# Second output projection: the order in which weight slabs are split and the residual is worked on

## What is computed

```python
merged = jax.nn.sigmoid(ga) * (ya @ w_branch_a[l]) + jax.nn.sigmoid(gb) * (yb @ w_branch_b[l])
h = h + merged @ w_out[l]                                     # the second output projection
h = h + 0.5 * swiglu(rms_norm(h, ffn2_norm[l]), ffn2_w_gate[l], ffn2_w_up[l], ffn2_w_down[l])
```

## Time and profile before

| | us |
|---|---|
| median of 3 runs | 1691.95 |
| lowest, highest | 1689.49, 1692.52 |
| the profiled execution, whole | 1687.92 |
| its span (first to last instruction) | 1686.0 |
| PE busy in the span | 1656.9 |
| DVE busy | 1038.9 |
| ACT busy | 738.2 |
| POOL busy | 177.9 |

### The profile page before, as it was taken

The page is one execution under the profiler, slowest core; times in us unless marked ns, Lnnn a source line. Parts: engine busy times, 40 slices in busy tenths (PEclk is TensorE's granted clock), DMA queues, the critical chain, the costliest instruction groups (busy, mean ns, idle before and its releaser), DMA issues.

```text
span 1686.0 us, 24849 instructions
## 1 busy us (share of the span) xinstructions
PE 1656.9 (98%) x9737; PEld 1415.5 (84%) x9737; DVE 1038.9 (62%) x1594; ACT 738.2 (44%) x1246; POOL 177.9 (11%) x185
## 2 busy tenths in 40 slices
PE   7999999999999998999999999999999999999998
PEld 5777687888888888989999887777888899998997
DVE  4888856443343376866767635666455687586773
ACT  3565644222222274524445422555444554253553
POOL 0120210020000012010000231002001200101102
PEclk9999999999999999999999999999999999999999
DMA  9733136373243378484565146112336975537721
GB/s 335 242 128 120 44 116 212 105 195 98 68 134 100 109 175 183 106 203 123 156 159 153 49 131 121 52 57 67 88 94 167 225 174 137 147 83 199 176 88 51
DMA packets 291463, 226.27 MB, mean 134 GB/s; under 512 B 16251, under 2 KB 275767, under 8 KB 291335
## 3 DMA queue, kind: packets, MB, share of 16 engines
q1 hardware_dynamic: 261056, 181.43, 34.6%
q0 software_dynamic: 29936, 43.18, 14.3%
q10 hardware_dynamic: 360, 0.13, 0.0%
HBM read 215.27 MB, written 6.36 MB: 131 GB/s over the span
## 4 chain that ended last, share of the span: by engine, by line
PE 56%; DVE 2%; ACT 1%; DMA 1%; issue 1%; POOL 0%; DVEq 0%; ACTq 0%; POOLq 0%
PE psum L698 10%; PE psum L700 10%; PE psum L699 10%; PE psum L1044 8%; PE psum L1047 8%; PE psum L1046 8%; PE psum L1192 1%; PE psum L1157 1%; DMA acc<-sq 1%; PE psum L1212 1%; DVE ring_lo L2211 0%; DVE w_lo L1971 0%; ACT ring_hi L1645 0%; DVE part_raw L2219 0%; PE psum L1130 0%
## 5 line engine op out<-in xcount | busy, mean ns | idle before, releaser
L2211 DVE TENSOR_TENSOR ring_lo<-part_raw,ring_hi 128x1024 fp32r<-128x1024 f32 (+1 forms) x270 | 323.4, 1199 | 200.6 <-ACT ring_hi L1645 199.7
L1645 ACT ACTIVATE ring_hi<-part_raw 128x1024 fp32r<-128x1024 f32 (+1 forms) x270 | 278.6, 1036 | 362.0 <-PE psum L700 286.3
L1044 PE MATMUL psum<-hq_hi,ring_hi 128*128 128x256 f32 x1232 | 350.3, 284 | 1.7 <-ACT t_gate L1736 1.2
L1046 PE MATMUL psum<-hq_lo,ring_hi 128*128 128x256 f32 x1232 | 349.1, 283 | 0.0
L1047 PE MATMUL psum<-hq_hi,ring_lo 128*128 128x256 f32 x1232 | 349.1, 283 | 0.0
L1044 PEld LDWEIGHTS psum<-hq_hi,ring_hi 128*128 128x128 f32 x1232 | 237.1, 192 | 3.0 <-issue 1.8
L1046 PEld LDWEIGHTS psum<-hq_lo,ring_hi 128*128 128x128 f32 x1232 | 237.1, 192 | 0.2
L1047 PEld LDWEIGHTS psum<-hq_hi,ring_lo 128*128 128x128 f32 x1232 | 237.0, 192 | 0.0
L698 PE MATMUL psum<-hid_hi,ring_hi 128*128 128x512 f32 (+1 forms) x536 | 207.2, 386 | 0.0
L699 PE MATMUL psum<-hid_lo,ring_hi 128*128 128x512 f32 (+1 forms) x536 | 206.9, 386 | 0.0
L700 PE MATMUL psum<-hid_hi,ring_lo 128*128 128x512 f32 (+1 forms) x536 | 206.8, 386 | 0.0
(11 more groups left out here) (305 smaller groups left out, 2418.7 us busy)
## 6 DMA issues: line engine op xcount, KB each, us to landing
part_raw<-in_ffn_w_up SPq DMA_DIRECT2D x66, 512.0 KB, 5.6
w_raw<-in_w_in SPq DMA_DIRECT2D x50, 512.0 KB, 3.7
part_raw<-in_w_gate_up SPq DMA_DIRECT2D x44, 512.0 KB, 4.9
part_raw<-in_ffn_w_gate SPq DMA_DIRECT2D x44, 512.0 KB, 6.9
part_raw<-in_ffn_w_down SPq DMA_DIRECT2D x32, 512.0 KB, 5.1
part_raw<-in_ffn_w_gate POOLq DMA_DIRECT2D x22, 512.0 KB, 7.0
part_raw<-in_ffn_w_up POOLq DMA_DIRECT2D x22, 512.0 KB, 9.9
sq<-in_w_ada SPq DMA_DIRECT2D x20, 512.0 KB, 4.6
```

Of the source, the lines that this page charges most:

```text
L1044: pe.matmul(o, a_hi, b_hi, start=fresh, stop=False, skip_group_check=True)
L1046: pe.matmul(o, a_hi, b_lo, start=False, stop=False, skip_group_check=True)
L1645: act.activation(ring_hi[slot][:, 0:n], pool_raw[s_][b][:, 0:n], ACT.Identity).then_inc(f_high, 1)
L2211: dve.tensor_tensor(ring_lo[slot][:, 0:n], raw_[:, 0:n], ring_hi[slot][:, 0:n].bitcast(F32), ALU.subtract).then_inc(f_ready, 1)
```

## The change

In the loop over tiles of out2, the split of a slab moves one tile forward. Before, iteration i began with the split of slab i+1 on ACT and on DVE. Now iteration 0 still splits slab 1, and then each iteration i up to 5 splits slab i+2. On ACT this stands at the head of iteration i, ahead of the split for the FFN, of the wait for x and of the work on h; it waits until PE has left slab i, which is when tile i is complete. On DVE it stands right behind the addition to x of tile i, ahead of `combos`. Iterations 6 and 7 split no slab.

```diff
@@ ScalarE @@
             for i, n in enumerate(PAIRED):
-                if i < KD - 1:
-                    split_high(S_OUT2 + i + 1)
+                if i == 0:
+                    split_high(S_OUT2 + 1)
+                if i < KD - 2:
+                    split_high(S_OUT2 + i + 2)
                 if i in AHEAD:
                     high(FIRST_ITEM[2] + AHEAD.index(i))
                 wait_new("out2", i, None, 1)
@@ VectorE @@
             for i, n in enumerate(PAIRED):
-                if i < KD - 1:
-                    split_low(S_OUT2 + i + 1)
+                if i == 0:
+                    split_low(S_OUT2 + 1)
                 b = wait_filled(dve, ("out2", i))
                 dve.tensor_tensor(x[:, n, :], psum[:, b, :], x[:, n, :], ALU.add).then_inc(x_new, 1)
+                if i < KD - 2:
+                    split_low(S_OUT2 + i + 2)
                 combos(n, "ffn2", NEW_X["out2"] + i + 1, col_of("ffn2_norm_2", n, None, 1),
                        lambda: lower(FIRST_ITEM[2] + AHEAD.index(i)) if i in AHEAD else None)
             lower(FIRST_ITEM[2] + 3)
```

## The result

| | before | changed |
|---|---|---|
| median | 1690.96 us (5 runs) | 1699.59 us (5 runs) |
| lowest to highest | 1689.49 to 1692.52 | 1697.87 to 1700.2 |
| profiled execution, span | 1686.0 | 1696.3 |
| PE busy | 1656.9 | 1661.3 |
| mean granted clock of PE | 0.997 | 0.992 |

The ratio on record is 1.0038, with a 95% interval of 1.0021 to 1.0055: slower, where the forecast was no change, and outside the range of 1688.0 to 1695.6. The medians differ by 8.6 us; their quotient is 1.0051, inside the interval but not the recorded ratio.

What follows compares the result with a forecast made beforehand. PE was taken to bound the kernel, with POOL's path nearly as long: -4.15 (stalls) + 1.05 (slab 7) + 3.0 (gather wait) + 0.9 (clock) = +0.8 us, so 1692.8 against the median 1691.95; range 1688.0 to 1695.6.

Steps and rivals of the forecast that it cites:

- the two paths: Up to 1345.09 us, PE's own path and one from the squares through POOL's queue were claimed nearly equal in length.
- The stalls of 4.15 us: PE's waits for late slabs in the out2 stage, claimed to cost 4.15 us and to go with the change.
- The split on PE's path: In out2, a split would end 2.5 us after its tile, against 5.44 for the next tile: no stall if slabs landed.
- slab 3: Its load would land only at 1295.1, holding ACT and DVE in its split; gather 1 moves from 1296.75 to 1300.75.
- the lag: Lateness of ACT, DVE and POOL after slab 3's split; DVE's falls over later tiles, tile 6 added at about 1323.3.
- The stall ahead of slab 7: Square of tile 4 waits for gather 2, delaying slab 7's split: PE stalls 0.9 us, plus 0.15 in slow matmuls.
- "POOL's order stays, and I take the durations of its DMAs unchanged.": POOL's gathers and adds keep order and durations; its path stays equal within 0.1 us, PE's gather wait grows to 3.6.
- slab 6 and POOL's adds: Slab 6, now issued at 1302.5 ahead of the adds at 1305.0, was taken to load in under 8 us, not 10.6.
- The bounds: Slab 6 at 10.6 us delays the last gather 1.4; slab 3 later adds 0.5; faster POOL gains 1.2; clock 0 or 1.1.
- rival (b), slower by late slabs: Slab 6 or 7 still moving blocks ACT in out2: +3.0 to +4.6 us, about 1695.6; chance 0.11.
- The clock: After PE's 3.6 us wait for the last gather, a lower clock costs 0.9 us net, 1.1 less 0.2 of idle time.
- The size: Whole kernel: +0.8 us in sum, a forecast of 1692.8 us against the median of 1691.95.

Runs made afterwards that it cites:

- e1: Changed kernel, with SP's loads of the weight pieces of FFN unit 1 held until gather 5 is done; ratio 1.0058.
- e7: Kernel before, with slabs 2 and 3 split in the old place and only slabs 4 to 7 one tile sooner; ratio 1.0036.
- e9: e7 with weight pieces B22 and B21 of FFN unit 1, and SP's loads behind them, held until the last gather is done; ratio 0.9982.
- e13: Changed kernel, with B22, B21 of FFN unit 1 and the loads behind them held until the last gather is done; ratio 0.9999, 1692.31 us.
- e14: Kernel before, with only the hold of B22, B21 and the loads behind them until the last gather is done; ratio 0.9986, 1688.51 us.
- e12: Kernel before, with the last gather moved ahead of the adding transfers of unit 1 in POOL's queue; ratio 0.9984.
- e10: e7 with the last gather moved ahead of the adding transfers of unit 1 in POOL's queue; ratio 0.9994.
- e11: e10 with B22 and B21 of FFN unit 1 also held until the last gather is done; ratio 0.9976, median 1687.8 us.
- e15: Kernel before, splits in the old place, with POOL starting gather 1 only when tile 2 has been squared; ratio 1.0027.
- e3: Changed kernel, with ACT's last square put behind its first copy for the FFN unit; ratio 1.0067.
- e4: Changed kernel, with 45 and 40 useless transposes in PE's queue ahead of its two long waits in the first FFN unit; ratio 1.0063, 1700.47 us.

## Why the prediction was wrong

*What bounds, the two paths.* Right. The stalls of 4.15 us were there to be had, 3.3 came, and a second path through POOL's queue of nearly equal length decided.

*The split on PE's path, slab 3, the lag.* Right to some tenths. Less the 0.64 us of offset: split of slab 3 at 1295.2 (forecast 1295.1), gather 1 at 1300.9 (1300.75), adds at 1304.9 (1305.0), gather 3 at 1317.3 (1317.5), square of tile 4 at 1317.05 (1317.3), tile 6 added at 1323.06 (1323.3), end of the stage at 1325.56 (1325.75). The stall ahead of slab 7 was 0.3 us (0.9).

*"POOL's order stays, and I take the durations of its DMAs unchanged."* This is the step that failed. The prediction said itself that the weight pieces of unit 1 come free sooner, and went no further: it never put the time of these loads (behind slab 7's split) beside those of the gathers. On its own numbers the split ended at 1320.1, so three loads of 512 KB would start at 1320.2, and gather 4, by its own walk at 1321, would run in them. Gathers 4 and 5 took 7.5 and 7.0 us instead of 3.2 and 3.3, 8 us together, of which less than one was slack; the sum came 7.75 us later. The prediction's last paragraph does say that it would be wrong in size if the gathers take another time under the shifted loads, but gives this no price and no chance. e1 shows that the loads make these two gathers long (3.2 us each with all loads held), and e7, e9 and e13 that they set the time: the same splits with and without two of those loads differ by 0.54% and 0.39%, of which the hold gives 0.14% to the kernel before as well.

That such loads and gathers share something stands in the Trainium skill, "DMA: Bandwidth & Descriptors", section "Issuing engines are not separate DMA queues": transfers run on the same 16 engines and interleave, whoever started them. The traces agree, with 7.5 us against 3.2 for one gather of 256 KB. The prediction had used the same thought for slab 6 and POOL's adds, rightly (slab 6 landed in 3.9 us, where it took under 8), and not for the gathers.

*The bounds.* They held a faster POOL and late slabs, and no slower POOL. With a gather at the 4.5 us that gather 6 showed in the kernel before, a slow end would have been seen. The gathers of the FFN before took 4.4 to 8.6 us, but they move 512 KB each, twice as much. The rival (b), slower by late slabs, had the right sign and the wrong mechanism: slab 6 landed in 3.9 us.

*The clock.* Right in kind: it fell after both waits. The term was too small: 0.9 us net was forecast, and behind the sum 1.9 us net were lost; between e13 and e14 it is 2.3. The forecast counted 3 us at the low clock, and neither the matmuls of the sum nor the rest of the low stretch, which lasted to some 6 us behind 1353.47.

*The size.* The forecast of 1692.8 is near what the changed kernel takes once two loads are held (1692.31). That agreement is in part luck: in that run gather 4 is still long, the last gather is shorter than before, and the clock costs more than forecast.

## What to carry to other kernels

When a change lets a queue of loads start sooner, lay the new times of these loads beside the transfers of the other queues, and price each transfer that now meets them by one that did meet some, not by its own old duration. A chain of small transfers, each awaited, is hurt most: loads beside a gather doubled its time, while two of them could go out some 20 us later without a new wait of PE (e13), and to hold these back by a semaphore was worth more here than the shorter stage. And a stall that disappears is a gain only up to the next path of equal length; look for it in the same profile, at the next wait of the bounding engine.

## What the runs showed of the hardware

- An accumulating DMA of 256 KB landed 3.2 to 3.6 us after its issue with no load of 512 KB issued near it. With three such loads issued 0.5 us behind it, it took 4.5 (before, e12), and 5.0 with a single one there (e14). With three or more issued 0.7 to 3.4 us ahead, it took 6.3 to 8.3 (changed kernel, e1 to e7, e10), but 5.1 once at 3.3 us (e7); with two issued up to 1 us ahead, 6.1 and 6.7 (e13, e11); with one 1.1 and 1.5 us ahead, 4.0 and 3.6 (e9, e13).
- Behind two accumulating DMAs of 512 KB, one of 256 KB lands 8.5 to 8.6 us after its own issue with no loads issued beside the three (e9, e13, e14). With loads issued 5.0 us behind the first of them it took 10.2 (before), 3.5 us behind 11.3 (e15), 1.7 us behind 11.8 (changed kernel), and from 0.7 us ahead to 0.4 us behind 13.4 to 14.4 (e7, e3, e1).
- PE's granted clock fell to 0.50 to 0.52 after waits of 4.96, 4.40 and 2.88 us, and not after 0.60. It was back at 1.00 some 4 to 6 us after the matmuls began again. The length of the wait alone does not decide: it fell after 1.89 us in e4 and stayed at 1.00 around a wait of 3.00 us in e3.
- 42 transposes of 128x128 in PE's queue kept the clock at 1.00 from 1335 to 1340 us in e4, where the changed kernel waited and fell to 0.55.
